# Two split activation tiles take another place in the on-chip memory: behind the work area instead of behind the ring of weights and x

## The chip, the cores and the metric

The kernel runs on one core of one Trainium2 chip, as one launch. The metric is the time of that launch on the device in microseconds (us), as the median of several runs. Of the kernel before there are three runs: 2167.13, 2170.5 and 2170.79 us.

## What is computed

The reference is two transformer stacks, one behind the other, over 256 tokens of width 1024, in float32. The first stack has two layers. Each is half a gated feed-forward (width 2816), a mixer, and half a feed-forward again; the mixer of layer 0 is chunked gated linear attention, that of layer 1 is multi-head latent attention, and both have a cross-attention into 256 memory tokens beside them:

```
x = x + 0.5 * swiglu(rmsnorm(x, g1), w_gate, w_up, w_down)
o = mixer(rmsnorm(x, gm) @ w_in);  o_mem = memory_cross_attention(...)
x = x + concat([o, o_mem]) @ w_out
x = x + 0.5 * swiglu(rmsnorm(x, g2), w_gate, w_up, w_down)
```

The second stack has two layers of retention and mLSTM side by side, merged by gates, with layer norms:

```
proj = x @ w_in                      # 8 200 columns, padded here to 33 x 256
y_ret = norm(retention(...)) * silu(r_g) @ w_proj_ret;  y_ml = ... @ w_proj_mlstm
x = layer_norm(a * x + (gate_a * y_ret + gate_b * y_ml) @ w_out)
x = layer_norm(a * x + (silu(gate) * up) @ w_down)
```

## The kernel before, in words

**Weights.** All weight matrices are cut on the host into 335 slots of 128 x 2048 float32 (1 MB). The slots pass one after the other through a ring of three buffers. SyncE issues one DMA for each into `raw`; ScalarE rounds it to the reduced float32 format that TensorE reads at one pass, `whi` (`act_hi`, line 225); VectorE computes the rest, `wlo = raw - whi` (`dve_lo`, line 230). A slot is free again when the products that read it have ended (`slot_used`).

**Activations.** They are kept transposed, features in partitions and 256 tokens in the free dimension, and they are split the same way: `in_hi` and `in_lo`, 12 blocks of 256 columns each, hold the rounded part and the rest of what goes into the next weight product; `h_hi` and `h_lo`, 2 blocks each, hold the hidden activations of a feed-forward pair.

**Products.** One weight block of 128 x 128 takes three matmuls of 256 columns (`pe_weight`, lines 234 to 236): `whi` by the high part, `whi` by the low part, `wlo` by the high part. The first operand is loaded into the array, the second one streams through it; each of the three has its own weight load. `pe_pair` runs 16 such blocks of a slot into one PSUM bank (48 matmuls); `pe_acc_slot` runs 16 blocks into four accumulator banks, for the down projection from `h_hi` and `h_lo`, for the last down projection of each feed-forward and for the output projection of the first stack from `in_hi` and `in_lo`. `pe_pairs_first` (lines 265 to 270) does the same work for the first two slots after a norm in another order. `pe_pair_tok` (lines 281 to 283) turns the roles round, where the result is wanted with tokens in partitions: a block of `in_hi` or `in_lo` is loaded, and 256 columns of `whi` or `wlo` stream. In the latent attention two chunks of values do so with 512 columns (lines 1170 to 1172).

**Feed-forward.** `pe_ffn` has a loop of nine rounds; a round is one gate slot and one up slot (2 x 48 matmuls streaming `in_hi` and `in_lo`) and one down slot (48 matmuls streaming `h_hi` and `h_lo`). There are six feed-forwards, so 54 such rounds. What lies before the first round and behind the last is written out. In the rest of the kernel the products of the mixers, the small float32 matmuls of norms and attention, and their evictions are ordered by hand, engine by engine, with semaphores.

**Where tiles lie.** `sb(...)` takes the next free bytes of each partition, in the order in which the tiles are declared, rounded up to 32 bytes. In the kernel before, `raw` begins at byte 16 512, `whi` at 41 088, `wlo` at 65 664, `x` at 90 240, `in_hi` at 98 432, `in_lo` at 110 720, then come `params` (123 008), `params2`, `lp`, `consts` (124 672) and the work area `ws` (137 472, 73 728 bytes), in which nearly all other tiles are views. Behind it lie `zeros` (211 200), `stat`, `small`, `eps`, and `h_hi` (213 536) and `h_lo` (215 584).

Of the kernel before, what the change touches and what calls it, by code (L numbers as in the profile page):

```python
# [19 lines left out]
F32R = mybir.dt.float32r  # L20
# [6 lines left out]
P = 128  # L27
T = 256
# [80 lines left out]
def build(nc, d_slots, d_x, d_mem, d_params, d_params2, d_consts, d_out):  # L109
    with ExitStack() as ctx:  # L110
        def sb(name, shape, dt=F32):
            return ctx.enter_context(nc.sbuf_tensor(name, shape, dt))
# [5 lines left out]
        whi = sb("whi", [P, RING, SLOT], F32R)  # L118
        wlo = sb("wlo", [P, RING, SLOT], F32R)
        x = sb("x", [P, DT, T])  # L120
        in_hi = sb("in_hi", [P, 12, T], F32R)
        in_lo = sb("in_lo", [P, 12, T], F32R)
        params = sb("params", [P, NPARAM])
        params2 = sb("params2", [P, LAYERS * NPARAM2])
        lp = sb("lp", [P, NPARAM2])
        consts = sb("consts", [P, NCONST])
        ws = sb("ws", [P, 9 * 2048])
        zeros = sb("zeros", [P, 512], BF16)
        stat = sb("stat", [P, T])
        small = sb("small", [P, 64])  # L130
# [2172 lines left out]
```

## Time and profile before

| | before |
|---|---|
| runs | 2167.13, 2170.5, 2170.79 us; median 2170.5 |
| span of the profiled execution | 2169.9 us |
| TensorE matmuls busy | 2102.8 us, 97% of the span, 16 726 matmuls |
| TensorE weight loads busy | 2048.3 us, 94% |
| VectorE busy | 1280.5 us, 59% |
| ScalarE busy | 1029.3 us, 47% |
| GpSimd busy | 122.1 us, 6% |
| mean granted TensorE clock | 0.992 of full |

The profiled execution has no time of its own beside its span, which is 2169.9 us. It lies between the lowest and the highest of the three runs, 0.6 us under their median. Busy time of TensorE is a union: matmuls overlap, one is in flight for some 280 ns while the next starts after some 120 ns. What a matmul costs is the distance from its start to the start of the next one, and that is read from a timeline, not from the mean duration.

### The profile page before, as it was taken

The numbers are of one execution on the slowest core, as the hardware profiler recorded it, in microseconds if no ns is written. First come the engines' busy times: TensorE is split into PE (matmuls) and PEld (weight loads), VectorE is DVE, ScalarE is ACT, GpSimd is POOL, SyncE is SP. The second block draws the span as 40 slices with busy tenths as digits, with TensorE's granted clock in tenths as the row PEclk, the third lists the DMA queues.
The fourth block names the chain that finished last, engine by engine and source line by source line (L and its number), as shares of the span: only waits on it lengthen the run. The fifth ranks groups of instructions, "written<-read, shape, count | busy, mean of one in ns | idle before, by whom it ended". The sixth has DMA issues, their size and how long they took to land.

```text
span 2169.9 us, 39735 instructions
## 1 busy us (share of the span) xinstructions
PE 2102.8 (97%) x16726; PEld 2048.3 (94%) x16748; DVE 1280.5 (59%) x1144; ACT 1029.3 (47%) x975; POOL 122.1 (6%) x83
## 2 busy tenths in 40 slices
PE   7999999999999999799999999999998999999997
PEld 6999998999999998599999999999998999999996
DVE  6556655655665567446557556665445566665445
ACT  5445645433444366434346454544435563545343
POOL 4000000100100002020000001010001000001001
PEclk9999999999999999899999999999999999999999
DMA  6555443455465444136454444535543444554452
GB/s 230 210 180 184 159 175 116 157 176 191 155 216 191 175 174 156 39 114 225 175 190 176 146 166 143 183 123 197 190 176 128 163 160 143 184 175 156 174 190 81
DMA packets 51562, 360.32 MB, mean 166 GB/s; under 512 B 5632, under 2 KB 7808, under 8 KB 8320
## 3 DMA queue, kind: packets, MB, share of 16 engines
q1 hardware_dynamic: 50768, 355.18, 45.7%
q0 software_dynamic: 688, 3.60, 0.5%
q8 instruction: 81, 1.33, 0.2%
q14 instruction: 25, 0.20, 0.0%
HBM read 357.71 MB, written 1.05 MB: 165 GB/s over the span
## 4 chain that ended last, share of the span: by engine, by line
PE 93%; DVE 3%; ACT 2%; issue 1%; POOL 1%; DMA 0%; ACTq 0%; SPq 0%; DVEq 0%; POOLq 0%
PE ps L234 25%; PE ps L235 25%; PE ps L236 25%; PE ps L282 2%; PE ps L281 2%; PE ps L283 2%; PE ps L265 1%; PE ps L270 1%; PE ps L266 1%; DVE wlo L230 1%; PE ps L583 1%; PE ps L1484 1%; PE ps L1476 1%; PE ps L1413 1%; PE ps L1437 1%
## 5 line engine op out<-in xcount | busy, mean ns | idle before, releaser
L230 DVE TENSOR_TENSOR wlo<-raw,whi 128x2048 fp32r<-128x2048 f32 x335 | 782.6, 2338 | 528.3 <-ACT whi L225 527.6
L234 PE MATMUL ps<-in_hi,whi 128*128 128x256 f32 x3708 | 1062.0, 286 | 11.6 <-DVE wlo L230 5.9
L235 PE MATMUL ps<-in_lo,whi 128*128 128x256 f32 x3708 | 1051.5, 284 | 0.0
L236 PE MATMUL ps<-in_hi,wlo 128*128 128x256 f32 x3708 | 1051.3, 284 | 0.0
L225 ACT ACTIVATE whi<-raw 128x2048 fp32r<-128x2048 f32 x335 | 637.8, 1906 | 251.5 <-PE ps L236 225.8
L234 PEld LDWEIGHTS ps<-in_hi,whi 128*128 128x128 f32 x3708 | 713.6, 192 | 18.9 <-issue 4.6
L235 PEld LDWEIGHTS ps<-in_lo,whi 128*128 128x128 f32 x3708 | 713.7, 192 | 2.2 <-issue 1.4
L236 PEld LDWEIGHTS ps<-in_hi,wlo 128*128 128x128 f32 x3708 | 713.7, 192 | 0.0
L234 PE MATMUL ps<-h_hi,whi 128*128 128x256 f32 x960 | 269.9, 281 | 0.0
L235 PE MATMUL ps<-h_lo,whi 128*128 128x256 f32 x960 | 268.6, 280 | 0.0
L236 PE MATMUL ps<-h_hi,wlo 128*128 128x256 f32 x960 | 268.5, 280 | 0.0
L234 PEld LDWEIGHTS ps<-h_hi,whi 128*128 128x128 f32 x960 | 180.8, 188 | 0.7
L235 PEld LDWEIGHTS ps<-h_lo,whi 128*128 128x128 f32 x960 | 180.8, 188 | 0.2
L236 PEld LDWEIGHTS ps<-h_hi,wlo 128*128 128x128 f32 x960 | 180.5, 188 | 0.0
L460 ACT ACTIVATE h_hi<-ws 128x512 fp32r<-128x512 f32 x60 | 37.9, 632 | 198.9 <-PE ps L236 197.7
L281 PE MATMUL ps<-whi,in_hi 128*128 128x256 f32 x384 | 110.2, 287 | 0.0
L282 PE MATMUL ps<-wlo,in_hi 128*128 128x256 f32 x384 | 108.7, 283 | 0.0
L283 PE MATMUL ps<-whi,in_lo 128*128 128x256 f32 x384 | 108.6, 283 | 0.0
L511 DVE TENSOR_TENSOR h_lo<-ws,h_hi 128x512 fp32r<-128x512 f32 x60 | 41.5, 691 | 106.9 <-ACT h_hi L460 106.9
L454 ACT ACTIVATE ws<-ws 128x512 f32<-128x512 f32 x44 | 27.8, 632 | 152.4 <-DVE ws L495 152.3
L1689 ACT ACTIVATE ws<-ps 128x512 f32<-128x512 f32 x40 | 23.9, 598 | 121.1 <-PE ps L236 87.2
L282 PEld LDWEIGHTS ps<-wlo,in_hi 128*128 128x128 f32 x384 | 73.7, 192 | 0.4 <-issue 0.2
(251 smaller groups left out, 1740.3 us busy)
## 6 DMA issues: line engine op xcount, KB each, us to landing
raw<-in_slots SPq DMA_DIRECT2D x335, 1024.0 KB, 4.8
ws<-in_mem_t POOLq DMA_DIRECT2D x2, 1024.0 KB, 8.2
consts<-in_consts SPq DMA_DIRECT2D x1, 1600.0 KB, 13.2
consts<-in_consts POOLq DMA_DIRECT2D x1, 1472.0 KB, 6.5
x<-in_x_t SPq DMA_DIRECT2D x1, 1024.0 KB, 7.6
y_t<-x SPq DMA_DIRECT2D x1, 640.0 KB, 3.4
y_t<-x SPq DMA_DIRECT2D x1, 384.0 KB, 3.7
params<-in_params SPq DMA_DIRECT2D x1, 105.0 KB, 14.5
```

What stands on the lines that cost most here:

```text
L225: act.activation(whi[:, j], raw[:, j], ACT.Copy).then_inc(hi_ready, 1)
L230: dve.tensor_tensor(wlo[:, j], raw[:, j], whi[:, j].bitcast(F32), ALU.subtract).then_inc(lo_ready, 1)
L234: pe.matmul(out, whi[:, j, o:o + n], hi, start=start, stop=False, skip_group_check=True)
L235: pe.matmul(out, whi[:, j, o:o + n], lo, start=False, stop=False, skip_group_check=True)
L236: return pe.matmul(out, wlo[:, j, o:o + n], hi, start=False, stop=stop, skip_group_check=True)
L281: pe.matmul(o, a_hi, w_hi, start=(k == 0), stop=False)
L282: pe.matmul(o, a_hi, w_lo, start=False, stop=False)
L283: last = pe.matmul(o, a_lo, w_hi, start=False, stop=(k == DT - 1))
L454: act.activation(silu_t, src, ACT.Silu).then_inc(ffn_silu, 1)
L460: act.activation(flat(hi), hidden, ACT.Copy).then_inc(ffn_hh, 1)
L511: dve.tensor_tensor(flat(lo), hidden, flat(hi).bitcast(F32), ALU.subtract).then_inc(ffn_hl, 1)
L1689: act.activation(out, src, func).then_inc(evicted, 1)
```

## The change

The two declarations of `in_hi` and `in_lo` move from behind `x` to behind `ws`. No instruction, no semaphore, no order and no shape is touched.

```diff
         x = sb("x", [P, DT, T])
-        in_hi = sb("in_hi", [P, 12, T], F32R)
-        in_lo = sb("in_lo", [P, 12, T], F32R)
         params = sb("params", [P, NPARAM])
         params2 = sb("params2", [P, LAYERS * NPARAM2])
         lp = sb("lp", [P, NPARAM2])
         consts = sb("consts", [P, NCONST])
         ws = sb("ws", [P, 9 * 2048])
+        in_hi = sb("in_hi", [P, 12, T], F32R)
+        in_lo = sb("in_lo", [P, 12, T], F32R)
         zeros = sb("zeros", [P, 512], BF16)
```

By the rule of placing, `params`, `params2`, `lp`, `consts` and `ws` move down by the 24 576 bytes of the two tiles (`consts` to 100 096, `ws` to 112 896), `in_hi` comes to byte 186 624 and `in_lo` to 198 912. Everything up to `x`, and everything from `zeros` on, `h_hi` and `h_lo` among it, stays where it is.

## Rows read from the trace of the kernel before

**Rows 1.** The page: span, engines and the chain of waits.
```profile
span 2169.9 us, 39735 instructions
...
PE 2102.8 (97%) x16726; PEld 2048.3 (94%) x16748; DVE 1280.5 (59%) x1144; ACT 1029.3 (47%) x975; POOL 122.1 (6%) x83
...
PE 93%; DVE 3%; ACT 2%; issue 1%; POOL 1%; DMA 0%; ACTq 0%; SPq 0%; DVEq 0%; POOLq 0%
```

**Rows 2.** Groups by line: line, engine, tiles, shapes, count | busy us, mean ns | idle before.
```profile
L234 PE MATMUL ps<-in_hi,whi 128*128 128x256 f32 x3708 | 1062.0, 286 | 11.6 <-DVE wlo L230 5.9 <-DVE in_lo L305 3.2 <-DVE in_lo L438 2.5
...
L234 PE MATMUL ps<-h_hi,whi 128*128 128x256 f32 x960 | 269.9, 281 | 0.0
...
L281 PE MATMUL ps<-whi,in_hi 128*128 128x256 f32 x384 | 110.2, 287 | 0.0
...
L265 PE MATMUL ps<-in_hi,whi 128*128 128x256 f32 x224 | 56.9, 286 | 5.6 <-ACT in_hi L1506 3.3 <-ACT in_hi L434 1.8 <-ACT in_hi L2103 0.5
```

**Rows 3.** Timeline of matmuls (start us, duration us), a round of the loop and its neighbours.
```profile
98.11 0.28 PE L234 MATMUL ps<-h_hi,whi 128*128 128x256 f32 x1
...
103.63 0.28 PE L236 MATMUL ps<-h_hi,wlo 128*128 128x256 f32 x1
103.75 0.28 PE L234 MATMUL ps<-in_hi,whi 128*128 128x256 f32 x1
...
115.26 0.28 PE L234 MATMUL ps<-h_hi,whi 128*128 128x256 f32 x1
...
120.89 0.28 PE L234 MATMUL ps<-in_hi,whi 128*128 128x256 f32 x1
```

**Rows 4.** Timeline, an output projection's slots, which stream in_hi.
```profile
405.79 0.28 PE L235 MATMUL ps<-in_lo,whi 128*128 128x256 f32 x1
405.91 0.28 PE L236 MATMUL ps<-in_hi,wlo 128*128 128x256 f32 x1
...
406.51 0.28 PE L235 MATMUL ps<-in_lo,whi 128*128 128x256 f32 x1
```

**Rows 5.** Timeline, the first down slot of a feed-forward, behind the cleared banks.
```profile
417.41 0.81 PE L295 MATMUL ps<-zeros 128*128 128x512 bf16 x3
...
418.18 0.28 PE L235 MATMUL ps<-h_lo,whi 128*128 128x256 f32 x1
...
423.76 0.28 PE L234 MATMUL ps<-in_hi,whi 128*128 128x256 f32 x1
```

**Rows 6.** Timeline, an in_hi block loaded and whi or wlo streaming, 256 columns.
```profile
788.47 0.28 PE L282 MATMUL ps<-wlo,in_hi 128*128 128x256 f32 x1
...
799.62 0.28 PE L282 MATMUL ps<-wlo,in_hi 128*128 128x256 f32 x1
```

**Rows 7.** Timeline, the same with 512 columns.
```profile
866.55 0.40 PE L1170 MATMUL ps<-whi,in_hi 128*128 128x512 f32 x1
866.79 0.39 PE L1171 MATMUL ps<-wlo,in_hi 128*128 128x512 f32 x1
867.02 0.40 PE L1172 MATMUL ps<-whi,in_lo 128*128 128x512 f32 x1
867.25 0.39 PE L1170 MATMUL ps<-whi,in_hi 128*128 128x512 f32 x1
```

**Rows 8.** Timeline, plain float32 sums of x and of the work area.
```profile
1644.93 3.72 PE L1476 MATMUL ps<-x,consts 128*128 128x256 f32 x16 [0.96 <-DVE x L1471]
1650.10 3.72 PE L1484 MATMUL ps<-ws,consts 128*128 128x256 f32 x16 [1.45 <-ACT ws L1497]
```

**Rows 9.** Windows: busy us (count) of each engine, granted clock, DMA share, GB/s.
```profile
98.11:103.75 5.64, 5.64 (x51) 5.64 (x49) 2.98 (x2) 1.92 (x1) 0.00 (x0) 1.00 0.54 193
103.75:115.26 11.51, 11.51 (x98) 11.51 (x97) 6.66 (x5) 6.16 (x5) 0.00 (x0) 1.00 0.50 179
...
103.75:120.89 17.14, 17.14 (x146) 17.14 (x145) 9.64 (x7) 8.08 (x6) 0.00 (x0) 1.00 0.52 184
```

**Rows 10.** Groups by line and form, VectorE and ScalarE: writes of both tiles.
```profile
L511 DVE TENSOR_TENSOR h_lo<-ws,h_hi 128x512 fp32r<-128x512 f32 x60 | 41.5, 691 | 106.9 <-ACT h_hi L460 106.9
...
L511 DVE TENSOR_TENSOR in_lo<-ws,in_hi 128x512 fp32r<-128x512 f32 x6 | 4.2, 692 | 4.2 <-ACT in_hi L460 4.2
...
L460 ACT ACTIVATE h_hi<-ws 128x512 fp32r<-128x512 f32 x60 | 37.9, 632 | 198.9 <-PE ps L236 197.7 <-DVE ws L507 1.2
...
L460 ACT ACTIVATE in_hi<-ws 128x512 fp32r<-128x512 f32 x6 | 3.8, 633 | 20.9 <-DVE ws L507 20.9
```

**Rows 11.** Timeline, single steps on h tiles within a down slot.
```profile
99.88 0.28 PE L234 MATMUL ps<-h_hi,whi 128*128 128x256 f32 x1
100.00 0.28 PE L235 MATMUL ps<-h_lo,whi 128*128 128x256 f32 x1
100.11 0.28 PE L236 MATMUL ps<-h_hi,wlo 128*128 128x256 f32 x1
100.23 0.28 PE L234 MATMUL ps<-h_hi,whi 128*128 128x256 f32 x1
100.34 0.28 PE L235 MATMUL ps<-h_lo,whi 128*128 128x256 f32 x1
100.46 0.28 PE L236 MATMUL ps<-h_hi,wlo 128*128 128x256 f32 x1
```

## The prediction, made blind

> **What bounds the kernel now.** I read the page first. Its engine line has TensorE busy for 97% of the span, and the chain of waits runs through TensorE for 93% [rows 1]. So the time is the number of matmuls times the distance between two starts, plus some 70 us in which TensorE stands (2169.9 - 2102.8 = 67.1). The groups by line come next: the three lines of one weight product have 3708 matmuls each that stream `in_hi` or `in_lo`, and 960 each that stream `h_hi` or `h_lo`; the reversed form has 384 a line, the first pairs after a norm 224 a line [rows 2]. The mean duration of the first kind is 286 ns, that of the `h` kind 281 ns, though line, shape, types and weights are the same. A duration is not a cost here, so I went to the timeline.
>
> There the difference is one of pace. 48 matmuls on `h` tiles start between 98.11 and 103.75 us, 117.5 ns apart; the 96 on `in` tiles up to 115.26 us are 119.9 ns apart; the next 48 on `h`, up to 120.89 us, 117.3 ns apart [rows 3]. The other rounds of the loop repeat this. The obvious innocent reason is that down slots write to four PSUM banks in turn and read their weight blocks in another order than gate and up slots. The output projection excludes it: it is the same helper as the down slot, but streams `in` tiles, and it goes from 405.79 to 406.51 us in six steps of 120 ns [rows 4]. What the other engines do is no reason either: VectorE is busy for 2.98 of 5.64 us beside `h` (53%) and 6.66 of 11.51 beside `in` (58%), and the DMAs are no rarer, 0.54 against 0.50 [rows 9]. So the tile that streams makes the difference, and the tiles differ in their address alone.
>
> **The change part by part.** Nothing is added or removed. Each edit moves bytes.
>
> (a) `in_hi` and `in_lo` as streamed operands: 3 x (3708 + 224) = 11 796 matmuls [rows 2]. They go from bytes 98 432 to 123 008 to bytes 186 624 to 211 200. The only streamed tiles of this type with another pace lie at 213 536 and above. If what makes `h` faster holds for the new place, each of them gains what `h` has. How much is that? In the loop 119.9 - 117.4 = 2.5 ns [rows 3]. In the first down slot of a feed-forward, which starts after a pause, 47 steps from 418.18 to 423.76 us give 118.7 ns, so 1.2 ns only [rows 5]; both paces are steady over their 48 matmuls. Six feed-forwards with nine rounds of 96 make 5184 matmuls that are in the surroundings of the first kind: 5184 x 2.5 = 13.0 us. The other 6612 stand in written-out code, often behind a pause: between 6612 x 1.2 = 7.9 and 6612 x 2.5 = 16.5 us, and I take 12. The sum is 25 us, with ends 21 and 30.
>
> (b) `in_hi` and `in_lo` as loaded operands, with the ring streaming: 3 x 384 = 1152 matmuls, 93 steps from 788.47 to 799.62 us at 119.9 ns [rows 6], and 24 of 512 columns at (867.25 - 866.55) / 3 = 233 ns [rows 7]. In the trace the pace follows the streamed tile, and here that stays low. I take 0; the ends are -3 us (1152 x 2.5) and +3.
>
> (c) `ws` and `consts` go down by 24 576 bytes. Sixteen plain float32 matmuls streaming `x` (byte 90 240) take 3.72 us, sixteen streaming the end of `ws` (byte 203 008) also 3.72 us [rows 8]. They need 216 ns each for 256 columns, so a few ns of delay would be covered in either place. 0.
>
> (d) VectorE and ScalarE write the moved tiles. The same instruction takes 691 ns into `h_lo` and 692 ns into `in_lo`, 632 ns into `h_hi` and 633 ns into `in_hi` [rows 10]. So address costs these engines nothing: 0, ends within 1 us.
>
> (e) Would the gain be given back? A round would shrink from 17.14 us by 0.24. VectorE needs 9.64 us of it and ScalarE 8.08, and DMA engines are busy for 0.52 [rows 9]; so there is room, and nothing is late next. The 67 us in which TensorE stands are norms and evictions and stay.
>
> From the profiled execution's span, 2169.9 - 25 = 2144.9; the median of the runs lies 0.6 us above that span, so I predict 2145 (rounded down from 2145.5).
>
> **A rule against it.** Two observations belong here. The first is that the row of 512 columns steps at 233 ns, while three bf16 matmuls of 512 columns take 0.81 us with the last one's tail, about 216 ns apart [rows 5, 7]. With weight loads of 128 columns beside both, it is the wide type whose stream is held up. The Trainium skill, TensorE: Matmul & The Clock Gate (Part 2: What happens when you issue a matmul), says the opposite: the array has two independent read ports, so loading the next weights takes nothing from the stream. SBUF — State Buffer (Who interferes with whom) likewise knows no address within a partition that makes TensorE slower. By these pages the change would give 2170.5; the trace disagrees with them in that two paces exist at all.
>
> **The rivals.**
> - *No effect.* What makes `h` different need not be how high it lies. Bytes 41 088, 65 664, 98 432 and 110 720 of the ring and the `in` tiles all leave 128 when divided by 1024: the two streams into TensorE begin at equal phase. `h` leaves 544, and it alone starts off a 64-byte boundary (32 over). The new home, 186 624 and 198 912, leaves 256: another phase, but still on 64 and on 128. If 64- or 128-byte phase is the cause, nothing changes: 2170.5. For it: in the `in` stretches every printed step is 0.12 us, as if locked, while `h` steps change between 0.11 and 0.12 [rows 4, 11]; that looks like two streams meeting at fixed places, and it has no need of a height. Against it: an off-boundary tile being the quicker one would be odd.
> - *Only the top.* The quick part may begin at 196 608 (192 KB). Then `in_lo` and three blocks of `in_hi` gain; a third of (a) and somewhat more: 8 to 10 us, 2161.
> - *Slower.* A phase of 128 bytes between the streams (256 against 128, modulo 512) may make them meet more often instead of less. The price is bounded by nothing nearer than the gap between the two paces, turned round: 11 796 x 2.5 = 29 us, 2200. It decides as soon as the mean step of lines 234 to 236 on `in` tiles goes over 120.4 ns (0.37 x 11 796 = 4.3 us).
> - *A larger gain.* If the new phase removes the meetings wholly, a 256-column step would be half of 216, 108 ns, and the weight load next to it would be the bound; at most 11 796 x 12 = 141 us, 2029. Nothing shows such a pace.
>
> **How the numbers follow.** The full gain by height gets 0.41, the top alone 0.08, the larger gain 0.04, no effect 0.35, slower 0.12. The likeliest is 2145, its own range 2138 to 2151. A change of 0.2% is 4.3 us, about what a measurement of this kernel can tell from none; so faster 0.53, same 0.35, slower 0.12. The range must hold both the gain and no effect, and leaves out the larger gain and most of the slower case: 2137 to 2173.
>
> **What would show it.** In the changed kernel's timeline, gate and up slots in the loop should step at 117 to 118 ns, a round should take 16.9 us instead of 17.14, and the means of lines 234 to 236 on `in` tiles should fall from 286 and 284 to about 281; lines 281 to 283 should stay. If `in` keeps its rigid 120 ns, height is not the cause and I am wrong; if only line 235 changes its pace, it is the top alone. If the paces change as foreseen but the time does not, something in (e) was missed.

## The result: 0.5% faster, by another mechanism than foreseen

| | before | changed |
|---|---|---|
| median of the runs | 2169.78 us (2167.13 to 2170.79) | 2159.56 us (2158.22 to 2160.99) |
| ratio | | 0.995, 95% interval 0.9938 to 0.9962 |
| span of the profiled execution | 2169.9 us | 2159.2 us |

The kernel gained 10.2 us where 25 were forecast. The page of the changed kernel, its engine line as in [rows 1]:

```profile
span 2159.2 us, 39735 instructions
...
PE 2091.3 (97%) x16726; PEld 2037.0 (94%) x16748; DVE 1280.7 (59%) x1144; ACT 1030.2 (48%) x975; POOL 121.9 (6%) x83
```

TensorE's busy time fell by 11.5 us and its idle time rose from 67.1 to 67.9; together that is the 10.7 us by which the span of the profiled execution is shorter. The busy times of VectorE, ScalarE and GpSimd moved by under 1 us. The groups by line, answering to [rows 2]:

```profile
L234 PE MATMUL ps<-in_hi,whi 128*128 128x256 f32 x3708 | 1059.5, 286 | 12.8 <-DVE wlo L230 6.4 <-DVE in_lo L305 3.2 <-DVE in_lo L438 3.1
L235 PE MATMUL ps<-in_lo,whi 128*128 128x256 f32 x3708 | 1049.1, 283 | 0.0
...
L281 PE MATMUL ps<-whi,in_hi 128*128 128x256 f32 x384 | 109.6, 285 | 0.0
```

The mean durations hardly moved. The pace, which here is the distance from one matmul's start to the next one's, did, as the timeline of one round of the feed-forward loop shows (start, duration; compare [rows 3]):

```profile
102.06 0.28 PE L234 MATMUL ps<-in_hi,whi 128*128 128x256 f32 x1
...
113.45 0.28 PE L234 MATMUL ps<-h_hi,whi 128*128 128x256 f32 x1
...
119.09 0.28 PE L234 MATMUL ps<-in_hi,whi 128*128 128x256 f32 x1
```

96 matmuls on `in` tiles take 11.39 us, 118.6 ns each (119.9 before), and a round takes 17.03 us instead of 17.14. Two more stretches tell against the forecast. In the reversed form, where the moved tile is loaded and the unmoved ring streams, the pace fell too: 94 steps from 222.33 to 233.49 us, 118.7 ns against the 119.9 of [rows 6]. And in a written-out stretch of the second stack the streamed `in` tiles, in their new home, still step at 120.0 ns (237 steps lie between the last two starts below):

```profile
222.33 0.28 PE L282 MATMUL ps<-wlo,in_hi 128*128 128x256 f32 x1
...
233.49 0.28 PE L283 MATMUL ps<-whi,in_lo 128*128 128x256 f32 x1
...
1301.73 0.29 PE L235 MATMUL ps<-in_lo,whi 128*128 128x256 f32 x1
...
1330.17 0.28 PE L235 MATMUL ps<-in_lo,whi 128*128 128x256 f32 x1
```

### The profile page after: what moved, and what is told of

It is laid out like the page before. It is cut to its first block, busy times and chain, and to the rows that moved or that the text cites. A ratio compares the mean times of both kernels' runs of the same rounds, so it can differ in the third digit from the quotient of the medians.

```text
span 2159.2 us, 39735 instructions
## 1 busy us (share of the span) xinstructions
PE 2091.3 (97%) x16726; PEld 2037.0 (94%) x16748; DVE 1280.7 (59%) x1144; ACT 1030.2 (48%) x975; POOL 121.9 (6%) x83
## 4 chain that ended last, share of the span: by engine, by line
PE 92%; DVE 3%; ACT 2%; issue 1%; POOL 1%; DMA 0%; ACTq 0%; SPq 0%; DVEq 0%; POOLq 0%
PE ps L234 25%; PE ps L236 25%; PE ps L235 25%; PE ps L282 2%; PE ps L281 2%; PE ps L283 2%; PE ps L265 1%; PE ps L270 1%; DVE wlo L230 1%; PE ps L266 1%; PE ps L583 1%; ACT whi L225 1%; PE ps L1484 1%; PE ps L1476 1%; PE ps L1413 1%
## 5 line engine op out<-in xcount | busy, mean ns | idle before, releaser
L234 PEld LDWEIGHTS ps<-in_hi,whi 128*128 128x128 f32 x3708 | 703.3, 190 | 21.0 <-issue 5.5
L235 PEld LDWEIGHTS ps<-in_lo,whi 128*128 128x128 f32 x3708 | 702.8, 190 | 2.2 <-issue 1.4
L236 PEld LDWEIGHTS ps<-in_hi,wlo 128*128 128x128 f32 x3708 | 702.9, 190 | 0.0
```

Source lines behind the costliest of these rows:

```text
L234: pe.matmul(out, whi[:, j, o:o + n], hi, start=start, stop=False, skip_group_check=True)
L235: pe.matmul(out, whi[:, j, o:o + n], lo, start=False, stop=False, skip_group_check=True)
L236: return pe.matmul(out, wlo[:, j, o:o + n], hi, start=False, stop=stop, skip_group_check=True)
```

## The experiments

All of them add unused tiles, so that others begin some bytes later; no instruction is touched. An element of such a tile has 4 bytes, so `[P, 32]` moves what follows by 128 bytes. "Low home" is the place of `in_hi` and `in_lo` in the kernel before, "high home" that in the changed one; `low_128` is the kernel before with the two tiles 128 bytes later, `high_384` the changed kernel with them 384 bytes later, and so on. Where they move within a home, as many bytes are added behind them as make 512 in all, so that `h`, and in the low home `ws` too, keep their phase, that is, their start modulo 512 or less. "Difference" means the start of the streamed tile less the start of the loaded one. The expectations weigh three ideas: the height of a tile in the memory, the phase of the two operands to each other, and whether a tile begins on a boundary of 64 or 128 bytes. In all of the runs but the last two `whi` and `wlo` begin at 128 modulo 256. The line numbers of `pe_weight` are 235 to 237 where a tile was added ahead of it in one place, 236 to 238 where in two, 237 to 239 where in three.

### Height against phase: low_128, high_384

```diff
 # low_128: the kernel before
+        pad0 = sb("pad0", [P, 32])
         in_hi = sb("in_hi", [P, 12, T], F32R)
         in_lo = sb("in_lo", [P, 12, T], F32R)
+        pad2 = sb("pad2", [P, 96])
 # high_384: the changed kernel, with 96 and 32 in their place
```

> The two tiles stay in their old, low home but begin 128 bytes later (98 560 and 110 848; 256 modulo 1024, as in the changed kernel); 384 unused bytes behind in_lo let all later tiles move by 512 together. Phase theory (the step depends on where the streamed and the loaded operand begin, modulo 512 or less): steps on in tiles 118.9 ns as in the changed kernel, time 2160. Height theory (the new place is what counts): 120.0 ns and 2170. Boundary theory (64 or 128 bytes): 120.0 ns and 2170.

> The tiles lie in the new, high home but 384 bytes further up (187 008 and 199 296), so that they begin at 128 modulo 512 like the ring, as in the kernel before. Phase theory: back to 120.0 ns and 2170. Height theory: 118.9 ns and 2160 as in the changed kernel.

Measured: low_128 2157.45 us, 0.9941 of before (0.9927 to 0.9955); high_384 2171.69 us, 1.0007 (0.9998 to 1.0016). First the timeline of low_128, then that of high_384:

```profile
101.90 0.28 PE L236 MATMUL ps<-in_hi,whi 128*128 128x256 f32 x1
...
113.18 0.28 PE L238 MATMUL ps<-in_hi,wlo 128*128 128x256 f32 x1
```

```profile
101.16 0.28 PE L236 MATMUL ps<-in_hi,whi 128*128 128x256 f32 x1
...
112.55 0.28 PE L238 MATMUL ps<-in_hi,wlo 128*128 128x256 f32 x1
```

These are 95 steps each: 118.7 ns in the old home and 119.9 in the new one. The whole gain of the change comes without the move, from 128 bytes, and goes away in the new home with 384. So height is not the cause.

### The phase of h given to in: low_416, high_288

The same edit with 104 and 24 elements in the low home, 72 and 56 in the high home.

> Low home, 416 bytes later (98 848 and 111 136), which is the phase of the h tiles, 544 modulo 1024. Phase theory: the in tiles take the pace of h, 117.4 to 118.7 ns, and the time falls to 2140 to 2155, below the changed kernel. Height theory: 120.0 ns and 2170.

> High home with the phase of the h tiles (186 912 and 199 200, 544 modulo 1024). Phase theory: the same as the low home with this phase, 2140 to 2155. Height theory: 2160, as the changed kernel. Both together (height and phase each have a part): less than either alone, under 2150 with the low one above it.

Measured: 2161.48 us, 0.9952 (0.9938 to 0.9966), and 2158.9 us, 0.9952 (0.9938 to 0.9966). The homes agree, but this is less than the 2140 to 2155 that the phase theory promised. A round of low_416:

```profile
103.31 0.28 PE L236 MATMUL ps<-in_hi,whi 128*128 128x256 f32 x1
...
114.69 0.28 PE L236 MATMUL ps<-h_hi,whi 128*128 128x256 f32 x1
...
120.39 0.28 PE L236 MATMUL ps<-in_hi,whi 128*128 128x256 f32 x1
```

The `in` tiles step at 118.5 ns, and the `h` tiles, whose phase had not been touched, at 118.8 (117.3 before). Yet of the 119 unbroken stretches (no step over 0.2 us) of 30 or more such matmuls on `in` tiles, 30 step at 117.3 to 117.6. So one and the same difference has two steady paces, and most sequences keep the one with which they came in. The 117.4 and 118.7 ns of the `h` tiles in the kernel before [rows 3, 5] are such a pair: both have the difference -96.

### The period, and h itself: low_256, h_96

```diff
 # h_96: the kernel before
+        pad0 = sb("pad0", [P, 24])
         h_hi = sb("h_hi", [P, 2, T], F32R)
```

> Low home, the in tiles 256 bytes later (384 modulo 512; the ring begins at 128 modulo 512). What counts is the difference between streamed and loaded operand. If it counts modulo 256 or less: locked at 120.0 ns, 2170. If modulo 512: another pace, 117.4 to 119 ns, 2145 to 2162.

> The in tiles as in the kernel before; only h_hi and h_lo move up by 96 bytes, to 128 modulo 512, the phase of the ring. Phase theory: the 2880 matmuls on h tiles lock at 120.0 ns too, 2880 x 2.5 = 7 us more, 2177. Height theory: h stays at 117.4, 2170.

Measured: low_256 2172.04 us, 1.0002 (0.9993 to 1.0012): 256 bytes are as none. h_96 2181.53 us, 1.0047 (1.003 to 1.0064): 96 bytes at the upper end of the memory make `h` as slow as `in`. Its timeline:

```profile
112.80 0.28 PE L234 MATMUL ps<-h_hi,whi 128*128 128x256 f32 x1
...
118.56 0.28 PE L234 MATMUL ps<-in_hi,whi 128*128 128x256 f32 x1
```

48 steps in 5.76 us are 120.0 ns, where [rows 3] have 117.3. The medians differ by 10 us, the spans of the two profiled executions by 8.6 (2178.5 and 2169.9). Summed over both traces, the steps on `h` tiles take 7.1 us more and those on `in` tiles in the loops 0.4; the rest is spread, and its cause is not shown.

### Other differences: low_64, low_32, low_64_lo_0

The edits are in the low home: 16 elements ahead and 112 behind; 8 and 120; and for the last run 16 ahead of `in_hi`, 48 between the two tiles, 64 behind.

> Low home, 64 bytes later. Phase theory: a pace of its own that need not be better; if 64 bytes were the grain, 120.0 ns and 2170, else between 117 and 119 ns and 2140 to 2160 for one direction (ring loaded, in streamed), and another pace in lines 281 to 283, where the roles are turned round and the difference is -64.

> Low home, 32 bytes later, off the 64-byte boundary as the h tiles are. If being off the boundary makes h quick: 117.4 to 118.7 ns, 2140 to 2160. If the difference of 96 bytes below the ring makes it quick: another pace, open; 2150 to 2172.

> Low home, in_hi 64 bytes after the ring's phase, in_lo at the ring's phase (difference 0 modulo 256). If each matmul has the pace of its own two operands: line 235 stays at 120 ns and lines 234 and 236 step at 117.5, mean 118.3, 2153. If one matmul sets the pace of the next (the offset between the two streams is carried on): all three lines at one pace, either 120 (2170) or 117.5 (2145).

Measured: low_64 2145.06 us, 0.987 (0.9853 to 0.9887); low_32 2144.32 us, 0.9871 (0.9855 to 0.9888). In low_64 the reversed form, whose difference is -64, had the quickest pace so far, 94 steps in 10.67 us, 113.5 ns:

```profile
222.59 0.28 PE L284 MATMUL ps<-wlo,in_hi 128*128 128x256 f32 x1
...
233.26 0.28 PE L285 MATMUL ps<-whi,in_lo 128*128 128x256 f32 x1
```

In low_32, 96 steps on `in` tiles take 11.20 us, 116.7 ns, while the `h` tiles between them, at -96 as ever, mostly go at 118.8:

```profile
101.39 0.28 PE L236 MATMUL ps<-in_hi,whi 128*128 128x256 f32 x1
...
112.59 0.28 PE L236 MATMUL ps<-h_hi,whi 128*128 128x256 f32 x1
```

Being off a 64-byte boundary is not what counts, since low_64 is on one and gains as much. low_64_lo_0 took 2159.29 us, 0.995 (0.9935 to 0.9964), between the two forecasts 2153 (each matmul at its own pace) and 2170 (all at the slow one):

```profile
105.09 0.29 PE L238 MATMUL ps<-in_lo,whi 128*128 128x256 f32 x1
105.22 0.28 PE L239 MATMUL ps<-in_hi,wlo 128*128 128x256 f32 x1
105.34 0.28 PE L237 MATMUL ps<-in_hi,whi 128*128 128x256 f32 x1
105.45 0.28 PE L238 MATMUL ps<-in_lo,whi 128*128 128x256 f32 x1
...
106.52 0.29 PE L238 MATMUL ps<-in_lo,whi 128*128 128x256 f32 x1
```

Twelve steps in 1.43 us are 119.2 ns. Behind the matmul on `in_lo`, the tile at difference 0, the step is at times 0.13; the others are at 0.11 to 0.12. Over the whole trace (steps under 0.2 us) the step behind a matmul on `in_lo` has a mean of 121.5 ns, behind the two on `in_hi` 117.8 and 117.0; in the kernel before the three means lie between 119.9 and 120.1. The delay sits with the tile that is in phase with the ring, and in the stretch shown it comes with every second one, in a pattern of six matmuls.

### The best difference: low_192, high_64, low_192_h32

48 and 80 elements in the low home; 16 and 112 in the high home, which is the changed kernel with 64 bytes more ahead of `in_hi`; and the first with 8 elements ahead of `h_hi` besides.

> Low home, in tiles 192 bytes later, which is 64 bytes below the ring modulo 256 (64 against 128). Where the reversed form had streamed minus loaded = -64 (lines 281 to 283 of the run with 64 bytes), it stepped at 115.8 ns. If only that difference modulo 256 counts: 115.8 ns on 11 796 matmuls, 48 us less, and 117.5 ns on the 1152 reversed ones: 2120. If the roles (ring streamed or ring loaded) matter besides: anything from 117 to 120 ns, 2140 to 2170.

> The changed kernel with 64 unused bytes ahead of in_hi: high home (186 688 and 198 976), difference -64 modulo 256 as the low home with 192 bytes. If the home is without effect: the same pace and the same time as that one, within 3 us. If height adds something of its own: a difference of over 4 us between the two.

> As the low home with 192 bytes, and h_hi and h_lo 32 bytes later, also to 64 modulo 256. If the difference alone counts: h goes from 117.5 to 115.8 ns, 2880 x 1.7 = 5 us below the run without it.

Measured: low_192 2118.06 us, 0.9747 (0.9733 to 0.9761); high_64 2115.02 us, 0.9739 (0.9727 to 0.9752); low_192_h32 2115.01 us, 0.9741 (0.9707 to 0.9775). All three are clearly faster than both kernels (the changed one has 0.995). The single runs scatter more than before: 2107.57 to 2119.05, 2111.67 to 2127.07, and 2100.09 to 2125.89 us. The traces show what goes with it. In high_64 the loop of the first feed-forward and that of the fourth:

```profile
102.63 0.28 PE L236 MATMUL ps<-in_hi,whi 128*128 128x256 f32 x1
...
113.81 0.28 PE L238 MATMUL ps<-in_hi,wlo 128*128 128x256 f32 x1
...
119.63 0.28 PE L236 MATMUL ps<-in_hi,whi 128*128 128x256 f32 x1
...
993.44 0.28 PE L236 MATMUL ps<-in_hi,whi 128*128 128x256 f32 x1
...
1004.21 0.28 PE L238 MATMUL ps<-in_hi,wlo 128*128 128x256 f32 x1
...
1009.96 0.28 PE L236 MATMUL ps<-in_hi,whi 128*128 128x256 f32 x1
```

The same code with the same addresses goes at 117.7 ns in one (95 steps in 11.18 us) and at 113.4 in the other (10.77 us), a round takes 17.00 or 16.52 us, and on the `in` tiles all nine rounds of a loop keep to one pace. Two of the six loops are quick in this execution, which took 2127.07 us, the longest of the six; all six are quick in the traced one of low_192, with 2107.57 us the shortest of its five. Of the unbroken stretches of 85 to 100 such matmuls, 34 of 76 and 73 of 78 are quick. So the two traces are ends, not middles, and the 19.5 us between their spans go with the paces: 15.0 of them are `in` steps in the loops. The clock does not tell the paces apart. First a slow and a quick round of high_64, then a quick one of low_192, with VectorE and ScalarE keeping up in all three (columns as in [rows 9]):

```profile
102.63:119.63 17.00, 17.00 (x147) 17.00 (x146) 9.64 (x7) 8.08 (x6) 0.00 (x0) 1.00 0.51 185
993.44:1009.96 16.52, 16.52 (x147) 16.52 (x145) 9.56 (x7) 6.80 (x5) 0.00 (x0) 1.00 0.56 191
```

```profile
99.06:115.58 16.52, 16.52 (x147) 16.52 (x145) 9.59 (x7) 8.09 (x6) 0.00 (x0) 1.00 0.54 190
```

In time the third edit can't be told from the first two, whose ratios lie in its interval. Its trace (2109.51 us) can be read all the same. `h` now has the difference -64 too, and takes the two paces of that difference:

```profile
110.10 0.28 PE L236 MATMUL ps<-h_hi,whi 128*128 128x256 f32 x1
...
115.54 0.28 PE L236 MATMUL ps<-in_hi,whi 128*128 128x256 f32 x1
```

These 48 steps take 5.44 us, 113.3 ns. In four of the six loops both kinds of tile go at 113.3, in the other two both at 117.8. The mean step on `h` falls from 117.4 ns in low_192's trace to 114.9, which is worth 7.1 us; the `in` tiles lose 7.2 us in the loops by the two slow ones.

### Difference or start: shift_64, ring_64

```diff
 # shift_64: the kernel before
+        pad0 = sb("pad0", [P, 16])
         raw = sb("raw", [P, RING, SLOT])
 # ring_64: the kernel before
         raw = sb("raw", [P, RING, SLOT])
+        pad0 = sb("pad0", [P, 16])
         whi = sb("whi", [P, RING, SLOT], F32R)
         wlo = sb("wlo", [P, RING, SLOT], F32R)
+        pad1 = sb("pad1", [P, 48])
         x = sb("x", [P, DT, T])
...
+        pad2 = sb("pad2", [P, 16])
         h_hi = sb("h_hi", [P, 2, T], F32R)
```

> 64 unused bytes ahead of raw: every tile begins 64 bytes later than in the kernel before, all differences are the same. If the difference between streamed and loaded operand counts: 120.0 ns on in tiles, 2170. If the start of the in tiles alone counts (now 192 modulo 256, as in the run with 64 bytes in the low home): 117.5 ns and 2145.

> whi and wlo begin 64 bytes later (192 modulo 256), in_hi and in_lo stay at 128 modulo 256 and h at its distance from the ring (-96). Difference streamed minus loaded is -64, as in the run with 192 bytes. If the difference counts: 113 to 116 ns on in tiles, 2105 to 2125. If the start of the in tiles counts: 120.0 ns, 2170.

Measured: shift_64 2170.07 us, 0.9997 (0.9985 to 1.001); ring_64 2119.27 us, 0.9761 (0.9737 to 0.9785). The `in` tiles of a gate and up slot in shift_64, 96 steps in 11.52 us, 120.0 ns:

```profile
100.84 0.28 PE L235 MATMUL ps<-in_hi,whi 128*128 128x256 f32 x1
...
112.36 0.28 PE L235 MATMUL ps<-h_hi,whi 128*128 128x256 f32 x1
```

One round of ring_64:

```profile
101.81 0.28 PE L236 MATMUL ps<-in_hi,whi 128*128 128x256 f32 x1
...
112.59 0.28 PE L238 MATMUL ps<-in_hi,wlo 128*128 128x256 f32 x1
...
118.33 0.28 PE L236 MATMUL ps<-in_hi,whi 128*128 128x256 f32 x1
```

The 95 steps on `in` tiles take 10.78 us, 113.5 ns, with `in` tiles that begin where they did modulo 256; four of the six loops have this pace, two go at 117.8. All starts moved together change nothing; the ring moved alone does what the `in` tiles moved alone did. It is the difference that counts.

### What the runs give together

Start of the streamed tile less start of the loaded one, modulo 256, and the paces of the long stretches (from their first and last starts, pauses left out; `in` and ring in both roles). "Reversed" is the form in which the ring streams, where the difference has the other sign:

| difference | ns per matmul of 256 columns | from |
|---|---|---|
| 0 | 119.9 to 120.0 | before, high_384, low_256, shift_64; h in h_96 |
| +32 | 116.6 to 117.8 | low_32 |
| +64 | 117.8, in low_64 9 of 120 stretches at 113.3 | low_64; low_192, high_64 and ring_64 reversed |
| +96 | 120.0 | low_416 and high_288, reversed form |
| 128 | 118.7 or 120.0 | changed kernel, low_128 |
| -96 | 117.3 or 118.7, some at 120.0 | low_416, high_288; h in most runs |
| -64 | 113.4 or 117.8 | low_192, high_64, ring_64; h in low_192_h32; low_64 reversed |
| -32 | 118.3 | low_32, reversed form |

## Why the prediction was wrong

**The reading held, the cause did not.** That the place of the tiles, and not the helper, the banks or the other engines, makes `h` quicker than `in` was right, and so was the way to weigh a nanosecond per matmul. The step that failed is the condition on which (a) rests: "If what makes `h` faster holds for the new place, each of them gains what `h` has." The two kinds of tile differed in their address alone, and I took the height of it. What counts is the difference to the operand loaded beside it, modulo 256, as low_128, high_384 and ring_64 show. In the kernel before it was 0, the slowest value; the move made it 128, because the tiles now lie 88 192 bytes further on (14 464 of parameters and constants, 73 728 of `ws`), 344 and a half times 256, and 128 gives 118.7 or 120.0. That `h` has -96 is where its 117.4 came from. The assumption in (b), that the pace follows the streamed tile, fell with it: in the reversed form only the loaded tile moved, and the pace went from 119.9 to 118.7 ns. That 2159.56 us lies within the stated range is no merit, since the range was made to hold both the full gain and no effect.

**Term by term.** Both traces have the same matmuls in the same order, so their steps can be subtracted one by one. (a) In the loops the mean step went from 119.9 to 118.7 ns, 6.3 us instead of 13.0. (b) The reversed form was put at 0; it gained 1.5 us. The 6612 matmuls in written-out code gained 2.6 us where 12 were expected: 5.4 by their pace, since some stretches stayed at 120.0, less 2.7 by longer pauses among them. Why the pauses grew is not shown; by 1 to 2 us they also differ between traces of one pace (high_384 and shift_64 against before). (c), (d) and (e) held: the steps on `h` and those of all other matmuls moved by about 0.1 us or less, the other engines' busy times by under 1, and rounds of 16.52 us in low_192 show that there was room for more than was forecast.

**The rivals.** "No effect" (0.35) was the nearest to the truth in its mechanism: it named the equal phase of the two streams and their locked steps. It failed in the grain: it took starts that agree modulo 64 or 128 for equal, where low_64, low_128 and low_256 show a period of 256, and so it gave 2170.5. "Only the top" gave 2161 and almost hit the time, by luck: in the changed kernel lines 234, 235 and 236 have one pace on `in` tiles (mean steps of 118.9, 119.0 and 119.0 ns), and in high_384 `in_lo` lies above byte 196 608 and the pace is 119.9. "Slower" did not come: 128 bytes between the streams gave 118.7 or 120.0 ns, not more than 120.4. The "larger gain" was held to be nearly impossible; the -64 runs went somewhat over a third of its way (some 55 of its 141 us). The remark that nothing shows such a pace came from a trace in which only two differences occurred.

**The rules of the Trainium skill** that were weighed ahead (TensorE: Matmul & The Clock Gate, Part 2, on two independent read ports; SBUF — State Buffer, Who interferes with whom) give no way for an address to change the pace. h_96 and low_192 disagree with that: 96 bytes cost 10 us, 192 bytes bring 54. Whether the two streams really meet somewhere, and where, was not measured; the runs show the difference of the starts as the cause, not the circuit.

## What to carry to other kernels

Where float32r matmuls of 256 columns follow each other with a weight load each, and TensorE is the bound, look at the distance between starts, not at durations, and at where both operands begin modulo 256 bytes. 64 unused bytes ahead of a tile (high_64, which adds 448 more behind to keep the rest in phase) brought 2% here over the changed kernel (ratios 0.974 and 0.995 to the kernel before). Before a tile is moved for its place, add a few unused bytes in the old place: if that does the same, place was not the cause.

## What was not expected of the hardware

The same code at the same addresses has two steady paces (113.4 and 117.8 ns at -64; 118.7 and 120.0 at 128), and the `in` tiles of a loop keep one of them over its nine rounds, some 150 us. The `h` tiles need not: in three loops of high_64 they change between 117.4 and 118.7 from round to round. The granted clock is 1.00 of full at either pace. Where the difference is -64, whole runs scatter by up to 26 us (low_192_h32), against 6 us of the kernel before beside these (2168.59 to 2174.57). What decides which pace is taken, and how to force the quicker one, stays open.
